# The low parts of every second column of the experts' first weights move from VectorE to GpSimd

## The reference

```python
s = jnp.einsum('thpd,hpkd->thpk', q, subkeys)           # 8 heads, 2 sets of 128 keys
s_top, i_top = lax.top_k(s, K)                          # K = 16
c_top, c_idx = lax.top_k(cand, K)                       # best 16 of 256 sums
e = i1 * N_KEYS + i2
g = jax.nn.softmax(c_top, axis=-1)
act = jax.nn.gelu(jnp.einsum('thkd,td->thk', ue, xb))   # ue = u[e]
return jnp.einsum('thk,thkd->td', g * act, ve)          # ve = v[e]
```

## Time and profile before

| | |
|---|---|
| Median of 3 runs | 2360.54 us (2357.69 to 2362.79) |
| The profiled execution's own time | 2357.31 us |
| Its span, first to last instruction | 2356.0 us |
| Mean granted TensorE clock | 0.989 |
| Busy: PE, DVE, ACT, POOL | 2253.4, 1555.1, 795.5, 3.8 us |
| Hidden stage, first u_low to last large matmul | 393.9 to 1245.1 us |
| u_low L1384 | 128 instructions, 155.7 us busy |

### The profile page before, as it was taken

The page is one execution under the profiler, slowest core; times in us unless marked ns, Lnnn a source line. Parts: engine busy times, 40 slices in busy tenths (PEclk is TensorE's granted clock), DMA queues, the critical chain, the costliest instruction groups (busy, mean ns, idle before and its releaser), DMA issues.

```text
span 2356.0 us, 28160 instructions
## 1 busy us (share of the span) xinstructions
PE 2253.4 (96%) x10668; PEld 1759.6 (75%) x10668; DVE 1555.1 (66%) x3905; ACT 795.5 (34%) x1136; POOL 3.8 (0%) x6
## 2 busy tenths in 40 slices
PE   7999999999999999999999999999999998898899
PEld 5777878877877655555788888888888886677677
DVE  4464432878778999999426666676666665677444
ACT  4334432333233343333332222222222244434531
POOL 0000000000000000000000000000000000000000
PEclk9999999999999999999999999999999999999999
DMA  4221232444444364455557556556555622222032
GB/s 162 81 61 44 76 100 71 148 134 134 134 138 131 121 237 166 166 224 178 198 199 242 185 190 213 184 177 213 195 180 197 211 98 64 63 72 72 10 99 89
DMA packets 159640, 333.03 MB, mean 141 GB/s; under 512 B 14353, under 2 KB 47633, under 8 KB 158225
## 3 DMA queue, kind: packets, MB, share of 16 engines
q1 hardware_dynamic: 155328, 293.81, 38.1%
q10 hardware_dynamic: 4176, 37.42, 3.9%
HBM read 261.98 MB, written 69.21 MB: 141 GB/s over the span
## 4 chain that ended last, share of the span: by engine, by line
PE 67%; DVE 27%; ACT 4%; issue 2%; DMA 0%; SPq 0%; ACTq 0%; DVEq 0%
PE bank L301 16%; PE bank L303 16%; PE bank L302 16%; PE bank L1333 13%; DVE hot_part L1282 9%; DVE u_low L1384 4%; DVE hot L1280 3%; DVE match L1198 1%; DVE match L1192 1%; DVE picked L1201 1%; PE bank L1820 1%; DVE weights_low L294 1%; PE bank L1032 1%; DVE top_work L1140 1%; DVE best_at L1139 1%
## 5 line engine op out<-in xcount | busy, mean ns | idle before, releaser
L1333 PE MATMUL bank<-xn_low,u_high 128*128 128x512 f32 x1024 | 416.8, 407 | 0.0
L1333 PE MATMUL bank<-xn_high,u_low 128*128 128x512 f32 x1024 | 416.3, 407 | 0.0
L1333 PE MATMUL bank<-xn_high,u_high 128*128 128x512 f32 x1024 | 416.0, 406 | 0.0
L301 PE MATMUL bank<-v_high,w_high 128*128 128x512 f32 x1024 | 398.6, 389 | 1.3 <-DVE v_low L1539 1.3
L302 PE MATMUL bank<-v_low,w_high 128*128 128x512 f32 x1024 | 398.4, 389 | 0.0
L303 PE MATMUL bank<-v_high,w_low 128*128 128x512 f32 x1024 | 398.3, 389 | 0.0
L294 DVE TENSOR_TENSOR weights_low<-weights_raw,weights_high 128x1024 fp32r<-128x1024 f32 (+1 forms) x105 | 127.3, 1217 | 231.8 <-ACT weights_high L285 231.5
L1282 DVE TENSOR_SCALAR hot_part<-every_key,key_value,gate_part 128x128 f16<-128x128 f16 x1024 | 268.2, 301 | 0.0
L1384 DVE TENSOR_TENSOR u_low<-u_raw,u_high 128x1024 fp32r<-128x1024 f32 x128 | 155.7, 1217 | 151.4 <-ACT u_high L1355 150.9
L1561 DVE TENSOR_TENSOR x<-x,bank 128x512 f32<-128x512 f32 x256 | 166.5, 682 | 129.9 <-PE bank L303 126.6
L1489 ACT ACTIVATE v_high<-v_raw 128x2048 fp32r<-128x2048 f32 x64 | 122.7, 1917 | 333.4 <-PE bank L303 327.7
(11 more groups left out here) (322 smaller groups left out, 3192.9 us busy)
## 6 DMA issues: line engine op xcount, KB each, us to landing
u_raw<-in_peer_u SPq DMA_DIRECT2D x128, 512.0 KB, 3.8
v_raw<-in_peer_v SPq DMA_DIRECT2D x64, 1024.0 KB, 5.3
weights_raw<-in_w_in SPq DMA_DIRECT2D x64, 512.0 KB, 3.7
hidden_scratch<-hidden SPq DMA_DIRECT2D x128, 256.0 KB, 2.2
gates_scratch<-gate_stage ACTq DMA_DIRECT2D x8, 4096.0 KB, 12.3
gate_in<-gates_scratch SPq DMA_DIRECT2D x256, 128.0 KB, 4.5
hidden_in<-hidden_scratch SPq DMA_DIRECT2D x32, 1024.0 KB, 7.8
weights_raw<-in_w_out SPq DMA_DIRECT2D x16, 512.0 KB, 3.6
```

What stands on the lines that cost most here:

```text
L301: engine.matmul(out, lh, rh, start=first, stop=False)
L1333: step = pe.engine.matmul(m.bank[b][:, :], left[:, k, :], right[:, k, :], start=(done == 0), stop=(done == 3 * KT - 1))
```

## The change

The odd columns' `u_low` is computed by GpSimd, in a new function `hidden_pool` that runs ahead of `two_pool` in GpSimd's stream. The instruction and its operands are the same. The semaphore `u_low` becomes two, one counted by DVE and one by GpSimd, and everyone who waited for `u_low` (PE ahead of a column, SP ahead of a load, SP at the start of the second block) now waits for the one of that column's parity.

```diff
+def low_ready(m, j):
+    return (m.s.u_low_pool if j % 2 else m.s.u_low_dve), j // 2 + 1
+
+def hidden_pool(m, p):
+    pool, s = m.pool, m.s
+    for j in range(1, N_KEYS, 2):
+        pool.wait_ge(s.u_high, j + 1)
+        pool.engine.tensor_tensor(p.u_low[j % U_PAIRS][:, :, :], p.u_raw[j % U_RAW][:, :, :],
+                                  p.u_high[j % U_PAIRS][:, :, :].bitcast(F32), ALU.subtract).then_inc(s.u_low_pool, 1)
...
 def hidden_sync(m, keep, p, following):
         if j >= U_RAW:
-            sp.wait_ge(s.u_low, j - U_RAW + 1)
+            sp.wait_ge(*low_ready(m, j - U_RAW))
...
 def hidden_tensor(m, keep, p, background, following):
-        pe.wait_ge(s.u_low, j + 1)
+        pe.wait_ge(*low_ready(m, j))
...
 def hidden_vector(m, keep, p, background, following):
     def split(j):
+        if j % 2:
+            return
         dve.wait_ge(s.u_high, j + 1)
         dve.engine.tensor_tensor(p.u_low[j % U_PAIRS][:, :, :], p.u_raw[j % U_RAW][:, :, :],
-                                 p.u_high[j % U_PAIRS][:, :, :].bitcast(F32), ALU.subtract).then_inc(s.u_low, 1)
+                                 p.u_high[j % U_PAIRS][:, :, :].bitcast(F32), ALU.subtract).then_inc(s.u_low_dve, 1)
...
 def two_sync(m, keep, w, combining):
-    sp.wait_ge(s.u_low, N_KEYS)
+    for j in (N_KEYS - 2, N_KEYS - 1):
+        sp.wait_ge(*low_ready(m, j))
...
     vector_program(m, keep, b, p, w)
+    hidden_pool(m, p)
     two_pool(m, w)
```

More of the change, by code:

```diff
@@ L118, in __init__ @@
         self.u_arrived = semaphores(nc, "u_arrived0 u_arrived1 u_arrived2 u_arrived3")
-        self.u_high, self.u_low, self.hidden_summed, self.hidden_out = semaphores(
-            nc, "u_high u_low hidden_summed hidden_out")
+        self.u_high, self.u_low_dve, self.u_low_pool, self.hidden_summed, self.hidden_out = semaphores(
+            nc, "u_high u_low_dve u_low_pool hidden_summed hidden_out")
         self.hidden_stored = semaphores(nc, "hidden_stored0 hidden_stored1 hidden_stored2")
```

## The result

The changed kernel takes 2377.05 us (median of 4 runs, 2375.47 to 2379.65), the kernel before beside it 2359.11 (2357.59 to 2362.79): 17.9 us more, ratio 1.0075 (95% interval 1.0057 to 1.0092). The prediction said 2378, which is 17.5 above the median of 2360.54 in the table; its sum was +19. The profiled execution took 2377.36 us with a span of 2376.0, 20.0 more than before.

A forecast was written before the change was run, and what follows sets the result against it. DVE was taken to bound the gates (8.446 us per column against PE's 7.75), PE nearly full elsewhere. Gates +21.9 and choice -3 gave +19 us; forecast 2378 us, range 2320 to 2400.

The forecast's parts named there:

- Likeliest case: Whole kernel: each GpSimd subtraction fully blocks DVE's fast instructions in the gates; +19 us, 2365 to 2402, chance 0.52.
- The relief of 1.13 us per odd column: Gates: each u_low that leaves DVE saves 1.13 us, 23.2 us in all; two columns then cost DVE 15.76 us.
- The return cost: Gates: each GpSimd subtraction costs DVE 2.2 us (bounds 0 to 2.7), so 45.1 us come back.
- The step that let the whole duration come back: Gates: DVE stands still for the whole 2.2 us of a subtraction, because the instructions met there are fast ones.
- +21.9: Gates: net loss in us, 45.1 coming back through blocking against 23.2 saved on DVE.
- -3: Choice: net gain in us, 0.9 sooner for each of four tiles; ends -12.9 without blocking, +19 with full blocking.
- 42%: Choice: share of DVE's work with two SBUF inputs, so 4.5 subtractions bring back 4.2 us against 5.1 saved.
- No clock is to be won there: Hidden stage, gates and the stretch after: granted clock already 1.00, so no gain from the clock.
- B: Whole kernel: no blocking, -23.2 us in the gates and -12.9 in the choice, 2321 to 2325; chance 0.34.
- C: Whole kernel: partial blocking, a subtraction costs DVE 1.1 to 1.5 us, -10 to +5 us; chance 0.08.
- D: Gates: DVE starves GpSimd until it waits for the next even u_high; +203 us, some 2560; chance 0.06.
- The waits of SP and the start of the stage: Hidden stage: SP's load waits for its column's low part, and the first subtraction has room; cost nothing.

The follow-up runs named there:

- experiment 3: Low parts of odd columns 67 to 109 not computed at all, otherwise the kernel before: 2335.75 us, ratio 0.9897 to the kernel before.
- experiment 8: Kernel before, but GpSimd makes low parts of odd columns 67 to 109, each in four instructions of 256 elements: 2376.95 us, ratio 1.0077.
- experiment 7: Kernel before plus 22 useless GpSimd memsets of 1024 elements per partition beside the gates: 2367.71 us, ratio 1.0037.
- experiment 1: Kernel before, but GpSimd makes low parts of odd columns 1 to 65 only, in the choice: 2352.71 us, ratio 0.9964.
- experiment 4: Kernel before, but GpSimd makes low parts of all columns 2 to 65, in the choice: 2340.02 us, ratio 0.9913.
- experiment 11: Changed kernel with another background pace (8 pieces in 5 columns for 48 columns, then 2 a column): 2381.69 us, ratio 1.0099 to the kernel before.

## Why the prediction was right

Likeliest case, sign and mechanism were right. That the size came out within 2 us is partly luck: the choice won 3.5 us more than forecast, while the gates with their aftermath cost 1.7 more and the part behind the hidden stage, which was in no term, 3.0.

*The gates stage.* The relief of 1.13 us per odd column, all on the path, is experiment 3 to the hundredth (15.77 against 15.76 for two columns). The return cost was taken as 2.2 us and is 2.12 to 2.19. Its make-up was a little different: GpSimd needs 2.39, not 2.2, and DVE loses some 0.2 us less than that: in the rows of 894 us the held instruction starts 0.11 us after GpSimd's and would have taken 0.16 us anyway. The step that let the whole duration come back holds, to these 0.2 us, for a subtraction, and not for a memset. +21.9 was forecast, and 20.0 up to column 108 was measured, with one more block and its aftermath of 3.6 behind that.

The Trainium skill, "SBUF — State Buffer", section "Who interferes with whom", describes a lock that is held for a whole instruction while the other engine fully blocks. The traces agree for GpSimd instructions that read: DVE is held for one instruction (experiment 8) and by its duration (2.07 to 2.19 us of 2.39). They don't agree for the memset of experiment 7, beside which DVE lost half of its duration. The section also says which DVE instructions are spared. The groups on DVE in the choice after the change, forms apart (count, busy us, mean ns), show it. Before, the means were, in the order of the rows, 1219, 418, 2289, 2278, 418, 281 and 288 ns:

```profile
L1399 DVE TENSOR_TENSOR u_low<-u_raw,u_high 128x1024 fp32r<-128x1024 f32 x34 | 44.6, 1311 | 86.2 <-ACT u_high L1368 86.0
L1198 DVE TENSOR_TENSOR match<-match,top_keys 128x256 f32<-128x256 f32 x64 | 28.4, 512 | 0.1
L1192 DVE TENSOR_TENSOR match<-digit_value,counting_sb 128x2048 f32<-128x2048 f32 x8 | 20.8, 2598 | 0.2
L1201 DVE TENSOR_REDUCE picked<-match 128x128 f32<-128x2048 f32 x8 | 18.3, 2283 | 0.2
...
L1166 DVE TENSOR_TENSOR candidates<-top 128x256 f32<-128x256 f32 x32 | 16.9, 570 | 0.0
...
L1136 DVE MAX8 top<-scores 128x8 f32<-128x128 f32 x64 | 15.2, 279 | 0.0
...
L1161 DVE CAST top_keys<-places 128x256 f32<-128x256 uint32 x4 | 3.0, 738 | 0.1
```

Two-input instructions and the cast are stretched on the mean; TENSOR_REDUCE and MAX8 with one input are not, to 5 ns.

*The choice.* -3 was forecast, as 0.9 us for each of four tiles less a little; -6.5 came in the profiled execution and -8.5 in experiment 1. The tiles did not share it. The first two stalls went whole. The chain before has

```profile
494.21 40.62 PE bank L1333 x179
...
582.92 40.34 PE bank L1333 x167
```

and after

```profile
491.12 84.38 PE bank L1346 x372
575.82 37.90 PE bank L1346 x167
```

so PE ends these 167 matmuls at 613.72 us where it was 623.26, 9.5 us earlier, of which 2.4 are the clock (37.90 us in place of 40.34). The third tile gave a part of that back, because blocks fell on its last steps, one of them on the eight match that had taken 2.69 us and one on the match L1192 that had taken 2.30:

```profile
646.66 4.87 DVE match L1198 x8
...
653.88 4.15 DVE match L1192
```

DVE was late with a low part of its own (PE's wait of 2.1 us for u_low) and then with `picked` (4.5 us, the longest). PE starts the third transposes at 664.33 us where it was 670.47, 6.1 us earlier, and the fourth at 750.96 where it was 757.47, 6.5 earlier. Together: PE's waits for `picked` fell by 6.3 us, the one for u_low took 2.1, the granted clock gave back an estimated 1.7 (after the change it is 0.72 over 12 us from 662 us and 0.86 from 751 us, so one of three dips is gone), and the stage began 0.4 us earlier, which makes 6.3 of the 6.5.

How often a block hits was put at 42%. By the rows above, the low parts, match, candidates and the cast took some 18 us more than before, 22% of the 82.4 us of the 33 subtractions up to 790 us. But the forecast counted only the 4.5 subtractions in the last 49 us before each transpose, and eight fall on a tile. So its 4.2 us of blocks per tile stand against 4.6 measured, near each other by luck. What the term had at nothing was the clock behind a stall, and the chance where a block falls. The waits for u_high did not shrink with every second low part gone (86.0 us between 400 and 790 us, 77.9 before); only in experiment 4, with all of them gone, did DVE work ahead (4.9 us), and no stall was left.

*The clock.* "No clock is to be won there" held for the two stretches named. In the gates after the change it falls to 0.95, and costs nothing there, since DVE is busy for the whole 346 us from 789 to 1135 and so never waits for PE. Behind column 108, where PE takes over, it does count: 0.86 from 1143 to 1155 us, by estimate 1.7 of the 3.6 us.

*The rivals.* B (no blocking) would have needed the picture of experiment 3. C needed a subtraction that costs DVE 1.1 to 1.5 us; it costs 2.07 or more, and only a copy or a memset costs less than C said. D, starvation, can be excluded: GpSimd started 0.11 us before the DVE instruction that it held, amid a train of instructions that overlap. Its longest subtraction took 4.2 us, and that shows the block from the other side: it started at 644.68 us, when DVE's two-input match L1192 had 2.0 us left, and took 1.8 us more than the usual 2.39. The waits of SP and the start of the stage cost nothing, as said.

## What to carry to other kernels

In this kernel, work moved from VectorE to GpSimd saved its time on VectorE and brought back GpSimd's own, nearly whole, where VectorE's stream consisted of the fast one-source instructions: with 1.13 us saved and 2.15 returned the move lost where VectorE bound, and cost nothing in the gates of experiment 11, where VectorE had slack. So decide by stage, and look at what VectorE runs there. And price a stall of TensorE above its length, since the clock was down behind three of four here; a wait that ties a background task to the main loop can be worth more than the instruction behind it.

## What the runs showed of the hardware that was not expected

- A GpSimd memset of 0.96 us delays a train of fast VectorE instructions by 0.45 us, about half its duration; a copy of 1.05 us by 0.87, a subtraction of 2.39 us by 2.15.
- The block works both ways: a subtraction of GpSimd that started with 2.0 us left of a two-input VectorE instruction took 4.21 us in place of 2.39.
- Four GpSimd subtractions of 256 elements take 2.90 us and cost VectorE 1.9; one of 1024 takes 2.39 and costs 2.1.
- Four stalls of TensorE, 12.9 us of waiting, cost 19.6 us: around three of them the granted clock is 0.72, 0.86 and 0.86 over 12 us.
